# A PEER layer stage on one core: low parts, late picks, dots and gate units placed anew in a hand-written order

## What is computed

```python
def peer(h, wq, subkeys, u, v):          # 8 heads, 16 of 16384 experts each, D_MODEL = 1024
    q = (xb @ wq).reshape(PEER_BLOCK, PEER_HEADS, 2, PEER_HALF)
    s = jnp.einsum('thpd,hpkd->thpk', q, subkeys)
    s_top, i_top = lax.top_k(s, PEER_TOPK)
    cand = s_top[:, :, 0, :, None] + s_top[:, :, 1, None, :]
    g_s, g_i = lax.top_k(cand, PEER_TOPK)
    e = jnp.take_along_axis(cand_idx, g_i, axis=-1)
    g = jax.nn.softmax(g_s, axis=-1)
    act = jax.nn.gelu(jnp.einsum('thed,td->the', u[e], xb))
    return jnp.einsum('the,thed->td', g * act, v[e])
```

## Time and profile before

| | |
|---|---|
| median of 3 runs | 2231.81 us (2225.08 to 2232.66) |
| the profiled execution, its own time | 2228.25 us |
| its span | 2226.6 us |
| PE busy | 2030.9 us |
| DVE, ACT, POOL busy | 1604.2, 854.5, 579.9 us |
| granted clock, mean | 0.954 of full |

### The profile page before, as it was taken

The page is one execution under the profiler, slowest core; times in us unless marked ns, Lnnn a source line. Parts: engine busy times, 40 slices in busy tenths (PEclk is TensorE's granted clock), DMA queues, the critical chain, the costliest instruction groups (busy, mean ns, idle before and its releaser), DMA issues.

```text
span 2226.6 us, 32324 instructions
## 1 busy us (share of the span) xinstructions
PE 2030.9 (91%) x10471; PEld 1637.8 (74%) x10471; DVE 1604.2 (72%) x3110; ACT 854.5 (38%) x1715; POOL 579.9 (26%) x599
## 2 busy tenths in 40 slices
PE   8998999669879999969899799979998999999997
PEld 7774576234446558869899789979997888888885
DVE  3563256775224346889999899989758999999988
ACT  1232022113202221124676476647853333333331
POOL 1000133332200000001222223223325555554540
PEclk9999899878989999989999899999999999999998
DMA  5333232997850231437799699969989999999992
GB/s 199 80 74 116 85 100 71 328 358 265 295 228 3 114 105 57 130 105 235 246 315 304 231 295 323 307 227 330 369 313 395 394 403 392 396 389 397 383 391 94
DMA packets 239937, 547.81 MB, mean 246 GB/s; under 512 B 22190, under 2 KB 122335, under 8 KB 238394
## 3 DMA queue, kind: packets, MB, share of 16 engines
q1 hardware_dynamic: 110714, 287.40, 36.7%
q0 software_dynamic: 60736, 208.40, 25.5%
q10 hardware_dynamic: 68352, 50.34, 6.9%
HBM read 485.58 MB, written 60.02 MB: 245 GB/s over the span
## 4 chain that ended last, share of the span: by engine, by line
PE 34%; DVE 18%; issue 6%; ACT 3%; DMA 2%; ACTq 0%; SPq 0%; DVEq 0%; POOLq 0%
PE psum L2805 22%; PE psum L2559 7%; DVE u_gather L2457 4%; PE psum L2116 3%; DVE hT L2485 2%; PE psum L2575 1%; DVE uL L2231 1%; DVE eq L2027 1%; ACT hT L2420 1%; DVE eq L2024 1%; DMA S<-activation_table 1%; DVE vecs L2028 1%; ACT uH L2363 1%; DVE cand L1989 1%; ACT hT L2415 1%
## 5 line engine op out<-in xcount | busy, mean ns | idle before, releaser
L2221 POOL DMA_INDIRECT u_gather<-in_u_rows,gather_ids x160 | 186.7, 1167 | 847.2 <-DVE dots L2457 497.2
L2559 PE MATMUL psum<-hH,uH 128*128 128x384 f32 x1024 | 354.3, 346 | 49.2 <-DVE uL L2231 49.2
L2559 PE MATMUL psum<-hH,uL 128*128 128x384 f32 x1024 | 346.4, 338 | 0.0
L2559 PE MATMUL psum<-hL,uH 128*128 128x384 f32 x1024 | 346.2, 338 | 0.0
L2805 PE MATMUL psum<-vH,wH 128*128 128x512 f32 x768 | 302.0, 393 | 11.3 <-DVE wL L2749 11.3
L2805 PE MATMUL psum<-vH,wL 128*128 128x512 f32 x768 | 300.9, 392 | 0.0
L2667 POOL DMA_INDIRECT v_gather<-in_v_rows,idx_now x160 | 236.9, 1481 | 245.8 <-DVE y_sample L2756 146.6
L2805 PE MATMUL psum<-vL,wH 128*128 128x512 f32 x768 | 300.7, 392 | 0.0
L2559 PEld LDWEIGHTS psum<-hH,uH 128*128 128x128 f32 x1024 | 195.3, 191 | 52.8 <-DVE uL L2231 52.4
L2457 DVE CUSTOM_DVE_ANT_0 u_gather<-u_gather,h 128x1024 f32<-128x1024 f32 x160 | 195.4, 1221 | 4.0
L2559 PEld LDWEIGHTS psum<-hL,uH 128*128 128x128 f32 x1024 | 195.7, 191 | 0.0
(11 more groups left out here) (510 smaller groups left out, 3331.5 us busy)
## 6 DMA issues: line engine op xcount, KB each, us to landing
u_raw<-in_uT SPq DMA_DIRECT2D x128, 512.0 KB, 5.3
S<-in_v_rows SPq DMA_DIRECT2D x64, 512.0 KB, 11.0
v_rest<-in_v_rows SPq DMA_DIRECT2D x64, 512.0 KB, 6.7
activation_table<-acts ACTq DMA_DIRECT2D x128, 192.0 KB, 4.6
gate_table<-Gtile ACTq DMA_DIRECT2D x48, 512.0 KB, 7.0
S<-gate_table SPq DMA_DIRECT2D x16, 768.0 KB, 7.3
S<-activation_table SPq DMA_DIRECT2D x16, 768.0 KB, 13.4
G_rest<-gate_table SPq DMA_DIRECT2D x16, 768.0 KB, 8.2
```

Source lines behind the costliest of these rows:

```text
L2221: c.nc.gpsimd.indirect_dma_start(c.ug[:, k % RG], None, c.A["u_rows"].rearrange("j i d -> (j i) d"), bass.IndirectOffsetOnAxis(ap=c.ids[:, ...
L2559: ins = nc.tensor.matmul(column[n % 4][:, 0:ND], w[:, n % RU, d], x[:, d], start=m == 0, stop=m == len(parts) - 1)
```

## The change

The constants change, and with them the order:

```diff
-STEP_COLS = ((2, 1) * 4, (5, 5, 5, 5, 5, 5, 4, 4), (5,) * 8, (4, 3) * 4)
-STEP_DOTS = ((1, 1, 1, 0, 0, 2, 2, 2), (6,) * 7 + (5,), (7, 6, 6, 6) * 2, (6,) * 8)
-TAIL_DOTS = (2, 1, 1, 1, 1, 0)
+STEP_COLS = ((2,) * 7 + (1,), (9, 4, 4, 4, 4, 3, 4, 3), (9, 5, 4, 4, 5, 4, 4, 5), (9, 3, 3, 2, 3, 3, 2, 3))
+STEP_DOTS = ((0, 0, 1, 1, 1, 2, 2, 2), (13, 4, 3, 3, 3, 3, 4, 3), (8,) + (5,) * 7, (7, 6, 7, 8, 7, 7, 8, 8))
+TAIL_DOTS = (3, 3, 3, 2, 2, 1)
```

In the routing ahead of the first column, six low parts are made by DVE between the parts of the last heads, and `columns` on DVE leaves those six out. The rounding of the first three columns on ACT moves into the last two passes of the scores. PE waits for the last scores itself, ahead of column 2:

```diff
@@ act_scores
-        for n in range(AHEAD):
-            act.wait_ge(c.u_in[n], 16)
-            nc.scalar.activation(uH[:, n], u[:, n], ACT.Copy).then_inc(c.u_hi, 1)
+            for n in (0,) if j == NJ - 2 else range(1, AHEAD) if j == NJ - 1 else ():
+                act.wait_ge(c.u_in[n], 16)
+                nc.scalar.activation(uH[:, n], u[:, n], ACT.Copy).then_inc(c.u_hi, 1)
@@ dve_scores
-            router.head(S0[:, keys], b.first, h, c.res0)
-            router.head(S[:, 0, keys], b.second, h, b.res)
+            for i in range(3):
+                router.part(S0[:, keys], b.first, h, c.res0, i)
+                if h == ROUTED - 1 and i == 1:
+                    low_u(c, dve, AHEAD)
+            if h == ROUTED - 2:
+                for n in range(AHEAD):
+                    low_u(c, dve, n)
+            for i in range(3):
+                router.part(S[:, 0, keys], b.second, h, b.res, i)
+                if h == ROUTED - 1 and i != 1:
+                    low_u(c, dve, AHEAD + 1 + i // 2)
@@ columns on DVE
-                    low_u(c, dve, n)
+                    if n >= AHEAD + 3:
+                        low_u(c, dve, n)
@@ columns on PE
+                    if n == 2:
+                        pe.wait_ge(c.s_ev, 4 * PH)
```

```diff
-                    for i in range(max(U_STEP, nc_, nd)):
+                    for i in range(places):
...
-                        if i < nd:
+                        for _ in range(i * nd // places, (i + 1) * nd // places):
                             dot(k)
...
-                        if gates and i == 1:
+                        if first and i < U_STEP:
+                            late_picks(p, i)
+                        if gates and i == 3:
                             tile_gates(p)
-                        if st == 0 and i == 4 and p:
+                        if first and i == 4:
                             slots_in(p)
+                        if first and i >= 6:
+                            for m in range((0, 2, 3)[i - 6], (2, 3, 4)[i - 6]):
+                                hots(p, st, m)
+                            for m in range((0, 1, 2)[i - 6], (1, 2, 4)[i - 6]):
+                                unit(p, st, m)
+                        if first and i >= 5:
+                            route(p, st, i - 5)
```

More of the change, by code:

```diff
@@ L2076, in score_programs @@
     s_mm, s_ev = c.sem("rs_mm"), c.sem("rs_ev")
+    c.s_ev = s_ev
     h_split, d_own = c.sem("h_split"), c.sem("score_dve")
@@ L2269, in gates_of, with steps @@
             return c.res0[:, 2] if p == 0 else b.res[:, 2] if p < STILE else c.resS[:, 2]
-        def steps(columns, dot, tile_pre, gates_out, tile_gates, slots_in, unit, route, flush):
+        def steps(columns, dot, tile_pre, gates_out, late_picks, tile_gates, slots_in, hots, unit, route, flush):
             n = k = 0
@@ L2281, in steps @@
                     nc_, nd = STEP_COLS[p][st], STEP_DOTS[p][st]
-                    routed, gates = st == (0 if p else 5), st == (0 if p else 7)
+                    routed, gates, first = st == (0 if p else 5), st == (0 if p else 7), st == 0 and p > 0
+                    places = max(U_STEP, nc_)
                     if routed:
                         tile_pre(p)
-                    for i in range(max(U_STEP, nc_, nd)):
+                    for i in range(places):
                         if i < nc_:
@@ L2336, in columns @@
                         sp.dma_start(u[:, n % RAW], A["uT"][n]).then_inc(u_in[n % RAW], 16)
-                steps(columns, *[nothing] * 8)
+                steps(columns, *[nothing] * 10)
                 sp.wait_ge(res_ready, STILE)
@@ L2438, in flush @@
                         store(NTB - 1, i)
-                steps(columns, nothing, nothing, gates_out, nothing, slots_in, unit, nothing, flush)
+                steps(columns, nothing, nothing, gates_out, nothing, nothing, slots_in, nothing, unit, nothing, flush)
             @block.vector
@@ L2542, in columns @@
                 def columns(n):
-                    low_u(c, dve, n)
-                steps(columns, dot, tile_pre, nothing, tile_gates, nothing, unit, route, nothing)
+                    if n >= AHEAD + 3:
+                        low_u(c, dve, n)
+                steps(columns, dot, tile_pre, nothing, late_picks, tile_gates, nothing, hots, nothing, route, nothing)
                 dve.wait_ge(c.dot_done, NDOT)
@@ L2577, in unit @@
                     ins.then_inc(g_mm, 1)
-                steps(columns, nothing, nothing, nothing, nothing, slots_in, unit, nothing, nothing)
+                steps(columns, nothing, nothing, nothing, nothing, nothing, slots_in, nothing, unit, nothing, nothing)
 FINAL = (0, 1, STILE, 2, 3)
```

13 lines of the change are left out of this document (6 added, 7 removed).

## The result

| | before | after |
|---|---|---|
| median of 4 runs each, same chip | 2232.17 us | 2208.64 us (2203.71 to 2212.51) |
| ratio, 95% interval | | 0.9902 (0.9882 to 0.9921) |
| the profiled execution, its span | 2228.25, 2226.6 us | 2211.67, 2210.0 us |
| from the end of the score matmuls to the last column's end | 711.8 us | 688.4 us |
| of that, PE's waits | 67.7 us | 45.1 us |

The change brings 1.0%. Forecast were 2.1%. The sign was right, and so was the mechanism of the early start and of the tile changes. The size was less than half of the forecast, because the term for DMA in the last tile was far too small. The time of 2208.6 us lies 1.6 us outside the range and 2.6 us from rival (a), in which DMA binds fully in the last tile.

What follows compares the result with a forecast made beforehand. PE was taken to bound the kernel, busy 2030.9 of 2226.6 us. Early start, tile changes and clock sum to -55 us, DMA adds 8, next stage 4: 2228 - 55 + 8 + 4 = 2185, stated 2184 us, range 2168 to 2207.

Steps and rivals of the forecast that it cites:

- the early start: Stage start: six low parts made during routing let PE start columns early; 19.5 us of idle become 6.6, -12.9 us.
- the tile changes: Gate tile changes: spread picks and later units cut PE idle from 8.3, 18.6, 18.6 to 6.3, 3.6, 3.6 us: -32.0 us.
- the term for DMA in the last tile: Last tile and tail: dots moved there make DMA slower than PE, +8 us, between 0 and 25.
- rival (a): Last tile: DMA binds fully at 382 GB/s with no lead, 34 us instead of 12, 2206 us; chance 0.20.
- Rival (c): Stage start: high parts wait for last scores or loads, PE starts only after routing, 2199 us; chance 0.08.
- rival (d): Ring of five gathers: denser gathers land in 13 us and hold DVE's dots, +71 us, 2244 us; chance 0.05.
- The clock term: Stage: shorter waits leave 9 of 19 us lost to lower clock, -10 us; 4 to 14 us left as bounds.
- The next stage: After the stage: first product waits longer for a reload behind the last gate stores, +4 us, between 0 and 9.
- the signs that were named for a wrong forecast: DVE idle before dots for gathers in the second tile; stage ending after 1640 us; lower clock through the first six columns.

Runs made afterwards that it cites:

- e3: After, with every gather from dot 88 on fetching half rows, 19 MB less, those dots not the reference's: 2186.65 us, 0.9807 of before.
- e9: After, with every second gate store of the units' loop issued from SP instead of ACT: 2205.45 us, 0.9894 of before.
- e8: After, with 44 of 48 gate stores issued from SP and 14 of the last tile's 58 dots in its first step: 2215.57 us, 0.9932 of before.
- e5: After, with 44 of the 48 gate stores issued from SP, six units later, instead of ACT: 2209.91 us, 0.9901 of before.
- e6: After, with 14 of the last tile's 58 dots in its first step, same bytes in the tile: 2213.26 us, 0.9907 of before.
- e12: After, with 14 dots moved from the last tile to tiles 1 and 2 and gate stores split between ACT and SP: 2208.92 us, 0.9908 of before.
- e4: After, with 14 dots moved out of the last tile, 7 each to tiles 1 and 2: 2203.97 us, 0.9860 of before.
- e7: After, with every second gather of dots 96 to 145 fetching half a row, 6.5 MB less, not the reference's dots: 2199.04 us, 0.9858 of before.
- e10: After, with 5.9 MB of gate stores moved from the last tile to tile 1, gathers untouched, table not the reference's: 2196.69 us, 0.9858 of before.
- e11: After, with 18 dots moved out of the last tile, 14 to earlier tiles, 4 to the tail: 2200.09 us, 0.9875; repeat 2201.35 us, 0.9864 of before.

## Why the prediction was off, point by point

**The early start: right.** The first column stands at 958.51 us, at once behind the scores, which in this execution ended 3 us later than before. The stalls ahead of columns 3 to 6 are 2.32, 1.03, 1.50 and 0.82 us (forecast 2.4, 1.3, 1.8 and, for the seventh low part, 1.1). The wait of PE for the last scores costs nothing. Tile 0 takes 88.0 us; forecast were 88.5. Rival (c) fell.

**The changes of the tile: right in kind, a little short.** Column 19 waits 1.81 us (forecast 2.7) and starts at 1046.49 us. The waits for the first unit are 3.05, 4.71 and 4.17 us against 3.1 each, and tiles 1 and 2 have waits of 5.3 and 7.6 us where 6.3 and 3.6 were forecast, column 19 counted to tile 1. The stalls of 9.32 us for `uL` are gone in both. No gather held DVE in tiles 1 and 2 for long; even late in the stage the loss was small (DVE's waits from 1420 to 1650 us: total, times, longest), so rival (d) did not come:

```profile
DVE u_gather L2476 <- DMA u_gather<-in_u_rows,gather_ids: 10.3, 12, 3.5
```

**The DMA term: the step that failed.** I had put +8 us for the last tile and priced it with 400 GB/s, a value between the mean of 382 and the slices of 419. Such a rate was sustained by no stretch of 100 us and more: the last tile of after ran at 347 GB/s (its repeat at 359), and before at 373 in a stretch in which PE hardly waited. The step took a value above the mean of a full stretch for its capacity, because single slices reach 419, although the same row has slices of 129 and 295. With 347 GB/s in place of 400 the forecast's own sum gives, as an estimate, 134.6 - 104 = 31 us for the tile and 35 - 25 = 10 us for the tail, and half of that is 20 us. With half the gather bytes (e3) 21 us come back, so the term is about +21 us instead of +8, at the upper end of the 0 to 25 that stood beside it. It is made of two parts: waits, 24.7 us in this tile instead of e3's 10.1, and lower clock, 23.9 us at the lower level instead of 10.2, which at half speed is another 7 us. I had allowed nothing of the clock to this term.

**The clock term: wrong in its sum, for the same reason.** I forecast 10 us won. Time at the lower level went from 49 to 41 us only, 4 us won. At the changes the forecast held: 0.93 to 0.94 instead of 0.85 to 0.91, 15.8 to 6.8 us in tile 1 and 18.4 to 10.2 in tile 2. But in the last tile it went from 10.2 to 23.9 us. The waits there, seven of 1.5 to 6.1 us, brought back what the changes had given.

**The account.** Forecast for the stage was 47 us less (12.9 + 32.0 + 10 - 8), measured are 23.4 (711.8 - 688.4). Of the missing 23.6, waits are 14.3 (45.1 against 20.1 + 2.7 + 8 = 30.8), of which 13.1 in the last tile (24.7 against 3.6 + 8). Half of these 13.1 remain in e3, which waits there for 10.1 us: they do not go with the bytes that e3 saved. The remaining 9 are work at the lower clock and small things (21.7 us against 12.6), in the main the last tile's.

**The next stage: right.** PE's wait for its first product is 9.28 us; it was 6.16. DVE's own wait for the reload is shorter than before, 9.95 us instead of 13.62, as its last dots end later; but the reload lands 6.6 us after the last column instead of 3.4, and that moves PE's first product. Forecast were 4 us. The whole of what is lost behind the stage is 20.5 - 16.6 = 3.9 us (end of the last column 1667.4 to 1646.9, execution 2228.25 to 2211.67); by the profile of after's repeat it is 6.2 us.

```profile
1656.17 0.80 PE L2828 MATMUL psum<-vH,wH 128*128 128x512 f32 x1 [9.28 <-DVE wL L2772]
```

**The weights.** Rival (a), DMA binding fully, is the one whose mechanism came, and I had given it 0.20 because PE hardly waited in the last tile of before. That was no evidence against it: before asked 361 GB/s there, after asks 396, and 373 was the mean of 128 us of it. That its 2206 us lie so near the measured time is in part luck: it had 18 + 7 + 9 = 34 us for the last tile, the tail and the next stage, where the runs show about 21 + 4. What fills the gap are waits that e3 keeps too, 10.1 us in the last tile and 7.2 in tile 2, where 3.6 and 3.6 were forecast. Of the signs that were named for a wrong forecast, one came: the stage ends at 1646.9 us, after 1640. Over its whole last tile, from 1480 to 1641 us, before moved 346 GB/s; at that rate the 59.0 MB of the new tile take 171 us instead of 149, an estimate that comes out at the measured loss, though stretches in which little was asked are part of that mean. The question to put was what the new tile asks, and against a mean, not whether the old tile waited. The Trainium skill, "DMA: Bandwidth & Descriptors", section "Where 436 GB/s comes from", gives about 358 GB/s for this direction, and I had set it aside because a row showed 382. As a ceiling the traces still contradict it (373 over 128 us in before). As the rate for this tile it would have served better than 400: the two profiles of after show 347 and 359, and the time by it, an estimate, was 2201 us. No run shows that the limit met here is the one that the page means, so the nearness may be chance.

**What stays open.** Why after moves less per second (347) at a share of 0.98 than before at 1.02 (373) was not found. Loads and gathers took longer per byte: in the two windows above a MB of gathers took 41.4 us of one DMA engine's time before and 43.8 after, a MB of loads 42.1 and 43.8, a MB of stores 49.9 and 50.0. It is no fixed property of the mix: with the bytes of after, its repeat moved 369 and e9 373 GB/s over the last 125 us of the tile. Nor is it shown why e9's profile has a last tile 11 us shorter without a gain in its time; one profile is one execution, and the two profiles of after itself differ by 4 us there. Nor why e8 is somewhat slower than e5 and e6, and e12 slower than e4. That bytes carry the loss rests on the timed ratios of e3, e7, e10 and of e11 with its repeats, not on these profiles.

## What to carry to other kernels

When work is moved from one stretch to another to cover a wait, add up what the receiving stretch then asks of DMA and hold it against the mean that a long, full stretch has sustained, not against the best slices. Allow for the clock as well: the waits that follow cost more than their own length (here 14.6 us of waits and about 7 us of lower clock). A stretch without waits says nothing of how much more it can take. And an early start is worth only what the slower engine can follow with: alone it gave 4 us of 19.5 (not told from none), with the work behind it taken away 11.

## What the runs showed of the hardware

- A DMA issue can hold the engine that makes it for 3.5 to 12.7 us when much is under way, with everything queued behind it on that engine. It is not bound to ACT: with the stores on SP, SP's issues took up to 4.8 us in e5 and 8.8 us in e8, and in e5 the loads came late.
- In mixed traffic of 192 to 512 KB loads and stores with gathers of 4 KB rows, stretches of 125 to 150 us with a share near 1 moved 335 to 373 GB/s; single slices of after reach 417, and lie also at 171.
- The DMA share does not tell how much room is left. The repeat of e11 has a share of 0.97 at 335 GB/s with few waits, after 0.98 at 347 with many. In e3, with half rows, the share is 0.91 at 292 GB/s: from after, the bytes per us fell by 16%, the share by 7%.
- Many short waits can come with as much lower clock as a few long ones. In the last tile, PE's waits and its time at the lower level were 24.7 and 23.9 us in after, in nine waits of at most 6.1 us, 22.1 and 17.9 in its repeat, 10.1 and 10.2 in e3, 9.4 and 6.8 in the repeat of e11; in tile 2 of before, with waits of up to 9.3 us, 25.8 and 18.4. In tile 0 of after, 5.7 us of waits of at most 2.3 us came with none.
